# Two-block kernel on one core: the second layer's unit order, the place of its norm's sums, and the loop order of the first output units

## What is computed

```python
def odd_mixer(h, w_in, conv_w, conv_b, w_rg, b_rg, w_ig, b_ig, lam, w_out):
    p = jnp.einsum("btd,dn->btn", h, w_in)
    xr, gate = jnp.split(p, [W_LRU], axis=-1)              # 12 heads of 128 each
    xc = causal_depthwise_conv(xr, conv_w, conv_b)         # 4 taps
    r = jax.nn.sigmoid(einsum("bthi,hij->bthj", xc_heads, w_rg) + b_rg)
    i = jax.nn.sigmoid(einsum("bthi,hij->bthj", xc_heads, w_ig) + b_ig)
    log_a = -LRU_C * r * jax.nn.softplus(-lam)
    a = jnp.exp(log_a)
    bterm = jnp.sqrt(-jnp.expm1(2.0 * log_a)) * (i * xc)
    _, hs = lax.associative_scan(_lin_combine, (a, bterm), axis=1)
    y = hs * jax.nn.silu(gate)
    return jnp.einsum("btn,nd->btd", y, w_out)
# the call: h = h + odd_mixer(rmsnorm(h, norm_odd), ...)

# end of the state-space mixer s5_mixer
    y = jax.nn.gelu(y)
    ab = y @ w_glu
    a, b = ab[..., :dm], ab[..., dm:]
    return a * jax.nn.sigmoid(b)
```

## Time and profile before

| | us |
|---|---|
| median of 3 runs | 1719.36 |
| lowest, highest | 1719.22, 1719.44 |
| the profiled execution | 1718.13 |
| its span, first to last instruction | 1716.2 |

### The profile page before, as it was taken

One profiled execution on the slowest core, in us unless ns is written; L12 is line 12 of the kernel. 1 busy time (PEld: TensorE's weight loads), 2 busy tenths in 40 slices (PEclk: granted clock), 3 DMA queues, 4 the chain that ended last, 5 costly groups with the idle time before them and its releaser, 6 DMA issues.

```text
span 1716.2 us, 20954 instructions
## 1 busy us (share of the span) xinstructions
PE 1691.8 (99%) x8056; PEld 1396.0 (81%) x8056; DVE 869.2 (51%) x1250; ACT 762.9 (44%) x1203; POOL 969.3 (56%) x606
## 2 busy tenths in 40 slices
PE   9999999999999999999999999999999999999998
PEld 7888888777778898888888888888678888888887
DVE  3999997757787785522212121386644221212124
ACT  5333325466867773343222222454765332323234
POOL 5858755657678565654444444664547444444464
PEclk9999999999999999999999999999999999999999
DMA  4322323222245234222222222223112222222221
GB/s 170 105 99 87 111 99 115 95 74 95 89 162 211 68 128 136 99 91 95 97 98 99 98 98 98 86 98 99 47 47 93 98 99 98 98 92 95 97 99 62
DMA packets 56258, 172.65 MB, mean 101 GB/s; under 512 B 6496, under 2 KB 14816, under 8 KB 55264
## 3 DMA queue, kind: packets, MB, share of 16 engines
q1 hardware_dynamic: 56160, 171.33, 29.5%
HBM read 165.01 MB, written 6.29 MB: 100 GB/s over the span
## 4 chain that ended last, share of the span: by engine, by line
PE 70%; DVE 5%; ACT 3%; issue 2%; POOL 1%; DMA 1%; SPq 0%; DVEq 0%; ACTq 0%
PE B L315 57%; PE B L1687 1%; PE B L2439 1%; PE B L2441 1%; PE B L2437 1%; PE B L2235 1%; PE B L2335 1%; PE B L2314 1%; DVE SW L1150 1%; PE B L298 1%; DVE B L1016 1%; PE B L1614 1%; PE B L1579 1%; PE B L300 1%; PE B L299 1%
## 5 line engine op out<-in xcount | busy, mean ns | idle before, releaser
L291 POOL TENSOR_TENSOR WL<-RAW,WH 128x1024 fp32r<-128x1024 f32 x281 | 681.8, 2428 | 613.6 <-ACT WH L287 613.3
L287 ACT ACTIVATE WH<-RAW 128x1024 fp32r<-128x1024 f32 x281 | 296.5, 1057 | 627.3 <-PE B L315 593.8
L315 PE MATMUL B<-P0h,WH 128*128 128x512 f32 x1096 | 428.1, 391 | 3.7 <-ACT WH L287 1.9
L315 PE MATMUL B<-P0l,WH 128*128 128x512 f32 x1096 | 421.9, 390 | 1.3 <-DVE P0l L432 1.3
L315 PE MATMUL B<-P0h,WL 128*128 128x512 f32 x1096 | 276.4, 389 | 0.0
L315 PEld LDWEIGHTS B<-P0h,WH 128*128 128x128 f32 x1096 | 205.7, 188 | 48.4 <-DVE Yl L428 2.6
L315 PEld LDWEIGHTS B<-P0l,WH 128*128 128x128 f32 x1096 | 205.8, 188 | 44.4 <-DVE P0l L432 2.3
L315 PEld LDWEIGHTS B<-P0h,WL 128*128 128x128 f32 x1096 | 205.7, 188 | 42.7
L439 DVE TENSOR_TENSOR H<-H,B 128x512 f32<-128x512 f32 x88 | 60.2, 686 | 288.3 <-PE B L315 288.2
L1967 DVE SCALAR_TENSOR_TENSOR TMP<-B,RS 128x512 f32<-128x512 f32 x64 | 44.1, 691 | 258.5 <-PE B L315 244.1
L315 PE MATMUL B<-P1h,WH 128*128 128x512 f32 x448 | 174.7, 390 | 0.0
(11 more groups left out here) (354 smaller groups left out, 2668.8 us busy)
## 6 DMA issues: line engine op xcount, KB each, us to landing
RAW<-in_w SPq DMA_DIRECT2D x281, 512.0 KB, 3.2
PX<-in_zeros SPq DMA_DIRECT2D x4, 1024.0 KB, 10.0
H<-in_xT SPq DMA_DIRECT2D x8, 256.0 KB, 4.8
U<-u SPq DMA_DIRECT2D x32, 64.0 KB, 2.0
g<-GB SPq DMA_DIRECT2D x8, 256.0 KB, 2.1
GB<-g SPq DMA_DIRECT2D x32, 64.0 KB, 2.0
out<-Q SPq DMA_DIRECT2D x4, 512.0 KB, 3.6
CA<-in_zeros SPq DMA_DIRECT2D x1, 1920.0 KB, 10.0
```

Of the source, the lines that this page charges most:

```text
L287: act.activation(WH[:, i % NS, :], RAW[:, i % NR, :], ACT.Copy).then_inc(*inc("w_hi", i))
L291: pool.tensor_tensor(WL[:, i % NS, :], RAW[:, i % NR, :], WH[:, i % NS, :].bitcast(F32), ALU.subtract).then_inc(*inc("w_lo", i))
L315: return pe.matmul(b[:, :], w[:, ws[c]], x[:, c, :], start=start, stop=stop)
```

## The change

Three edits. In `ODD`, the gate units G0 to G3 move forward among X7 to X11: the order becomes ... X5 X6 G0 X7 G1 X8 X9 R1 G2 X10 G3 X11 G4 G5 R2 ...; the sums of the norm are issued inside X1, after its first two chunks, by way of `between`, which `linear` calls after chunk n's first two products; and in `pe_glu_start` the loop over chunks becomes the outer one, with the three units inside. There, the waits for the three units' banks and low weights come ahead of the first matmul.

```diff
--- before.py
+++ after.py
@@ -46,7 +46,7 @@
 
 EVEN = ("G0 A0 G1 A1 B0 B1 B2 B3 G2 A2 G3 A3 S0 S1 S2 S3 P0 B4 B5 G4 A4 G5 A5 B6 S4 B7 S5 S6 S7 "
         "G6 A6 G7 A7 P1 F0 F1 F2 F3 F4 F5 F6 F7 K0 K1 K2 K3 K4 K5 K6 K7 O0 O1 O2 O3 O4 O5 O6 O7").split()
-ODD = ("X0 X1 X2 X3 X4 R0 X5 X6 X7 X8 X9 X10 X11 R1 G0 G1 G2 G3 G4 G5 R2 G6 G7 G8 G9 G10 G11 "
+ODD = ("X0 X1 X2 X3 X4 R0 X5 X6 G0 X7 G1 X8 X9 R1 G2 X10 G3 X11 G4 G5 R2 G6 G7 G8 G9 G10 G11 "
        "O0 O1 O2 O3 O4 O5 O6 O7 Q0 Q1 Q2 Q3").split()
 EVEN = [(x[0], int(x[1:])) for x in EVEN]
 ODD = [(x[0], int(x[1:])) for x in ODD]
@@ -804,7 +804,8 @@
             i = IDX[what]
             wh, wl = weights(i)
             if kind in "XG":
-                linear(pe, what, P0h, P0l, range(8), ("x_lo", ("xc" if kind == "X" else "y", c)), "odd" if n == 0 else None)
+                linear(pe, what, P0h, P0l, range(8), ("x_lo", ("xc" if kind == "X" else "y", c)), "odd" if n == 0 else None,
+                       {1: lambda: stat_sums(pe, "odd", pool=rbanks)} if n == 1 else {})
             elif kind == "O":
                 if c == 0:
                     banks.queue.extend(rbanks.queue)
@@ -837,9 +838,7 @@
                     last.then_inc(*inc("unit", what if j else ("q4", 2 * c)))
                     if (c, j) == (3, 0):
                         pe_square_sums(pe, (4, 5))
-            if (kind, c) == ("X", 0):
-                stat_sums(pe, "odd", pool=rbanks)
-            elif (kind, c) == ("X", 1):
+            if (kind, c) == ("X", 1):
                 stat_spread(pe, "odd", pool=rbanks)
 
     def unit_key_ri(r, h):
@@ -1804,19 +1803,18 @@
     def pe_glu_start(pe, chunks):
 
         for what in GLU[:3]:
-            i = IDX[what]
-            wh, wl = weights(i)
             if chunks[0] == 0:
                 _, before = banks.take(what, "evac_a" if what[2] > 7 else "evac_d")
                 pe.wait_ge(*at(*before))
-                pe.wait_ge(*at("w_lo", i))
-            b = banks.bank[what]
-            for c in chunks:
-                pe.wait_ge(*at("g_lo7" if c == 7 else "g_lo", ("g", c)))
-                ws = slice(128 * c, 128 * c + 128)
-                last = mm3(pe, b[:, :], wh[:, ws], wl[:, ws], P0h[:, c, :], P0l[:, c, :], c == 0, c == 7)
-            if chunks[-1] == 7:
-                last.then_inc(*inc("unit", what))
+                pe.wait_ge(*at("w_lo", IDX[what]))
+        for c in chunks:
+            pe.wait_ge(*at("g_lo7" if c == 7 else "g_lo", ("g", c)))
+            ws = slice(128 * c, 128 * c + 128)
+            for what in GLU[:3]:
+                wh, wl = weights(IDX[what])
+                last = mm3(pe, banks.bank[what][:, :], wh[:, ws], wl[:, ws], P0h[:, c, :], P0l[:, c, :], c == 0, c == 7)
+                if c == 7:
+                    last.then_inc(*inc("unit", what))
 
     def pe_glu(pe):
         pe_glu_start(pe, range(7, 8))
```

## The result

Six executions of the changed kernel took 1724.50 to 1727.09 us, median 1725.37; the kernel before, 1719.2 beside them. The ratio is 1.0037, with a 95% interval of 1.0027 to 1.0047: slower, by some 6 us. The forecast was 1721.5, at most 1723.8.

The account below looks back on a forecast made before the run. TensorE, busy 99% of the span, bounds the kernel, so only its pauses count: −1.8 + 2.8 + 1.1 = +2.1, from 1718.13 to 1720.2 us. Against the runs' median of 1719.36 the forecast was 1721.5, range 1717.4 to 1723.8.

Parts of the forecast that it names:

- The sums inside X1: Odd layer's norm: matmuls of X1 fill PE's wait for the squares, −0.9 us, bounds 0 and −0.97.
- X11 and R1: Odd layer: X11's 0.72 wait goes and R1's waits shrink from 3.96 to 2.2; R1 ends 2.45 us earlier.
- R2: Odd layer: DVE's moved taps make the second head wait 2.2 us; R2's waits total 3.0 instead of 1.3.
- The bound of -5.85: Odd layer with the norm: largest gain, every listed wait gone but 0.44 each at two heads.
- Rival (b): Odd layer: the order removes all waits, −5.85+2.8, giving 1716.3 us, or 1717.4 with the clock's price; chance 0.12.
- G10: Odd layer after R2: its 1.57 us wait stays, its chain following R2's end 0.75 to 1.0 earlier.
- The clock: Glu start: PE's clock falls to half inside the 4.3 us stop, costing +1.1 us, at most 2.1.
- The glu start: PE stands still for the third weight, +4.1 us; chunk 6's wait goes, −1.25; net +2.8, at most +3.3.
- The sum: Whole kernel: odd layer −1.8, glu start +2.8 and clock +1.1 make +2.1 us.
- Rival (d): Behind the glu stop: clock stays at half long after, through glu's chunks and y7; up to 1724.1 us; chance 0.11.

Follow-up runs that it names:

- 5: Kernel before with the norm's sums inside X1 alone; median 1717.11 us.
- 6: Changed kernel with POOL's sum for head 11 made ahead of the weights' low part, not behind it; 1721.99 us.
- 3: Changed kernel, but ahead of y7 the glu units run one after another, each waiting only for its own weights; 1717.85 us.
- 4: Kernel before with the new order of X and G units alone; 1720.84 us.
- 7: Changed kernel with 18 matmuls of constants put ahead of the wait for the third glu weight, filling the stop; 1723.84 us.
- 1: Changed kernel with the glu start put back as it was before; 1720.43 us.
- 11: 8 with the closing norm's sums issued one chunk at a time, though in Q3 three chunks came to stand together; 1715.83 us.
- 13: 8 with the closing norm's two-column sums spread, really one chunk at a time; 1715.92 us.
- 8: Kernel before with the sums inside X1 and the glu start with late waits, old unit order; 1715.67 us.
- 9: Changed kernel with both repairs: POOL's sum for head 11 ahead of the weights, and the glu start with late waits; 1716.28 us.
- 14: 9 with the closing norm's two-column sums spread one chunk at a time; 1716.51 us.
- 10: 8 with DVE's two tables (six operations) moved from behind R2 to behind G11; 1720.73 us.

## Why the prediction was wrong, point by point

- **The sums inside X1:** forecast -0.9, measured -0.85 at X2, and kept to the end in 5. Right.
- **X11 and R1:** X11's wait is gone; R1's waits cost 2.4, with 0.25 for each pause added, forecast 2.2. The gain at R2's start was 3.2 with the norm, forecast 3.35. Right.
- **R2:** waits of 2.09 and twice 0.18, 3.2 in all, forecast 3.0. Right; the list of DVE's work held. (The bound of -5.85 does not come out of the text: the waits that it lists, 0.9, 0.72, 3.96, 1.3 and 1.57, less 0.44 at two heads make 7.6. Rival (b) rests on it; nothing measured here turns on it.)
- **G10: the step that failed.** "... that chain follows R2's end, so it comes 0.75 to 1.0 earlier and the wait stays." It came 0.2 earlier: the chain starts 1.2 sooner, but takes 1.0 longer, because X11's move brings POOL's sum for head 11 beside DVE's tables. I had followed the queues of PE, DVE and ACT and not POOL's to this place, and POOL paced the chain before the change too. The odd layer's gain ahead of G10 was 0.3 (from +0.06 to -0.22), not 1.8: 1.5 of the miss. 6 undoes it.
- **The clock: mis-sized by its places.** I asked for it only at the stop of 4.3. It fell behind G10's wait of 2.30 as well (1.6) and at Q2 (1.55). The fall at Q2 was chance: the sums there are as they were, and the traces of 3, 4 and 6 have no fall at them. The text itself noted that 2.2 us without a matmul had been enough at the run's end, and then did not apply this to R2's wait of 2.1, which it forecast, or to the chance that G10's grows.
- **The glu start:** 4.15 from before it to the fourth unit, 2.8 and about 1.35 for the clock (7 measures 1.3); forecast 2.8 and 1.1. Right; chunks 6 and 7 do not wait. The Trainium skill's rule of program order ("TensorE: Matmul & The Clock Gate", "Step-by-step: what each phase is for") agrees: y7 starts behind the glu matmuls, and nothing fills the 4.25. The Trainium skill's Part 1 on the clock gate ("TensorE: Matmul & The Clock Gate", "Part 1: The HAM clock gate"), which lets idleness take PE to the half rate, agrees too: the granted clock was 0.50 behind the stop, 1.00 with the stop filled.
- **The sum:** 1.5 + 1.6 + 1.55 + 0.25 is 4.9, which with the forecast of 2.1 makes 7.0 of the 7.1 between the two profiled executions. Rival (d) had named the clock and the sign, but put it in one long stretch at the glu start. In the medians the miss is 3.9, since half of the executions of the kernel before have one fall as well: 13 of the 30 beside kernels 1 to 4 took 1717.5 to 1718.5 at a mean granted clock of 0.999, 17 took 1719.0 to 1720.1 at 0.997 to 0.998. Where it falls in those 17 no trace of the kernel before shows; 11 and 13 point to the closing norm's sums. The profiled one was of the first group, and I read the 1.2 between it and the median as a constant.

## What to carry to other kernels

Hoisting several waits to the head of a loop makes the first matmul as late as the last of them: change the order of a loop, and leave each wait where its data is first read (8 keeps the gain of the new loop and none of its loss). When work is moved, follow every queue to the new place, that of an engine off the critical path too: what stands behind a waiting instruction in it may wake beside the chain that matters. A DVE operation that is long only beside POOL is a sign of this; compare it with the same row where POOL rests. And on a kernel that keeps PE 98% busy, price a pause by what it does to the clock too: G10's wait of 2.3 cost 1.6 more behind it. Filling the stop of 4.25 (7) and splitting the two-column sums (13) kept the clock.

## What the runs showed of the hardware that was not expected

- All five traces with a wait of 2.3 at G10 (the changed kernel, 1, 3, 4, 7) show a granted clock of 0.50 behind it, and none of the nine with 1.3 does. R2's stop of 2.1 was followed by a fall in three of eight (1, 4, 7).
- A fall of TensorE's clock does not need an idle engine. 0.28 of idle time and 1.98 us of two-column matmuls came before it at Q2; split into parts of 1 us, no group of slower executions was left in 13.
- The same kernel falls in some executions and not in others, which splits its times into groups 1.1 to 1.7 us apart (medians of the groups in the kernel before, 5, 8, 9, 11 and 14). For changes of 0.1% the groups say more than the medians.
- DVE's operations on two tiles of SBUF were held by the POOL instruction that ran when they started. The five long rows of the changed kernel in 6 ended 0.55 after POOL's, one of them 2.78 instead of 0.69 long; with POOL at rest they took 0.7 (10). The scaling of 472.30, one input of which is in PSUM, took 0.69 beside a POOL subtraction. The Trainium skill ("SBUF — State Buffer", "SBUF: two separate sides") describes the ports that the two share as a lock held for a whole instruction. All five rows agree. So does POOL's own subtraction of 464.85: it began while DVE's operation of 463.66 was at work and took 2.85, where the one of 460.77 took 2.42.
